# Router on turned tiles of the residual between the output product's last steps, ranks in five wide matmuls, shorter slot sums, and attention evictions between weight splits

## The reference

```python
def first_block(x, ...):
    h = rmsnorm(x, norm1_g)
    u, v_a, q, k, v_b = jnp.split(h @ w_in, splits, axis=-1)
    y_a = chunked_spatial_gating(u, v_a, v_norm_g, w_s, b_s)
    q, k = rmsnorm(q per 64 columns), rmsnorm(k per 64 columns)
    o = rmsnorm(diff_attention(q, k, v_b, lam, slopes), sub_norm_g) * (1.0 - lam_init)
    g_a, g_b = jnp.split(jax.nn.sigmoid(h @ w_gate + b_gate), 2, axis=-1)
    merged = g_a * (y_a @ w_up_a) + g_b * (o @ w_up_b)
    x = x + merged @ w_out
    h2 = rmsnorm(x, norm2_g)
    return x + hierarchical_moe(h2, ...)

def hierarchical_moe(t, w_rg, b_rg, w_re, b_re, w1, w3, w2):   # 4 groups of 8 experts
    g_gate, g_idx = lax.top_k(softmax(t @ w_rg + b_rg), 1)
    e_logits = (t @ w_re + b_re)[the 8 of group g_idx]
    e_w, e_idx = lax.top_k(softmax(e_logits), 2)
    weight = g_gate * e_w / sum(e_w)
    y = sum over the 2 chosen experts of weight * (silu(t @ w1) * (t @ w3)) @ w2
```

## Time and profile before

| what | us |
|---|---|
| median of 3 runs | 1691.47 |
| lowest and highest | 1690.91, 1695.44 |
| the profiled execution | 1695.65 |
| its span, first to last instruction | 1693.9 |
| TensorE busy | 1515.3 (89%) |
| VectorE busy | 935.4 (55%) |
| ScalarE busy | 717.2 (42%) |
| GpSimd busy | 143.3 (8%) |

### The profile page before, as it was taken

The page is one execution under the profiler, slowest core; times in us unless marked ns, Lnnn a source line. Parts: engine busy times, 40 slices in busy tenths (PEclk is TensorE's granted clock), DMA queues, the critical chain, the costliest instruction groups (busy, mean ns, idle before and its releaser), DMA issues.

```text
span 1693.9 us, 17655 instructions
## 1 busy us (share of the span) xinstructions
PE 1515.3 (89%) x7159; PEld 1138.8 (67%) x7159; DVE 935.4 (55%) x1292; ACT 717.2 (42%) x1046; POOL 143.3 (8%) x87
## 2 busy tenths in 40 slices
PE   7999999899899647999999959896978999999999
PEld 5888776677678534555555538675867876678887
DVE  3544237754756356888888846656554453222344
ACT  4333334553452205666677653443221126643221
POOL 0000000000000001444333320000000000000000
PEclk9999989999999867999999989997978977999999
DMA  6222221131232607999999961201010012002231
GB/s 213 75 100 88 87 74 51 50 100 50 75 117 105 220 34 246 312 308 311 310 313 311 308 213 51 75 25 50 1 50 1 1 50 99 1 1 96 89 139 50
DMA packets 76955, 205.40 MB, mean 121 GB/s; under 512 B 10707, under 2 KB 11845, under 8 KB 72774
## 3 DMA queue, kind: packets, MB, share of 16 engines
q1 hardware_dynamic: 70978, 193.70, 33.6%
q0 software_dynamic: 5760, 10.50, 2.4%
q10 hardware_dynamic: 132, 0.03, 0.0%
HBM read 195.81 MB, written 16.78 MB: 125 GB/s over the span
## 4 chain that ended last, share of the span: by engine, by line
PE 63%; DVE 25%; ACT 9%; issue 1%; DMA 1%; SPq 0%; DVEq 0%; POOLq 0%; ACTq 0%
PE PS L501 15%; PE PS L503 15%; PE PS L502 14%; DVE wlo L1158 6%; DVE htlo L1158 5%; PE PS L934 4%; ACT whi L1957 3%; DVE ylo L1158 3%; PE PS L498 2%; PE PS L1083 2%; ACT yhi L1957 2%; ACT hthi L1957 2%; PE PS L1074 2%; ACT work L1957 1%; DVE work L1575 1%
## 5 line engine op out<-in xcount | busy, mean ns | idle before, releaser
L1158 DVE TENSOR_TENSOR wlo<-raw,whi 128x2048 fp32r<-128x2048 f32 x74 | 169.5, 2291 | 333.8 <-ACT whi L1957 333.8
L1957 ACT ACTIVATE whi<-raw 128x2048 fp32r<-128x2048 f32 x74 | 141.5, 1912 | 307.9 <-PE PS L503 296.6
L501 PE MATMUL PS<-hthi,whi 128*128 128x512 f32 x480 | 198.2, 413 | 10.0 <-DVE work L1283 6.4
L501 PE MATMUL PS<-whi,hthi 128*128 128x512 f32 x480 | 199.5, 416 | 8.2 <-ACT work L1957 6.4
L503 PE MATMUL PS<-whi,htlo 128*128 128x512 f32 x480 | 190.2, 396 | 0.0
L502 PE MATMUL PS<-wlo,hthi 128*128 128x512 f32 x480 | 189.9, 396 | 0.0
L503 PE MATMUL PS<-hthi,wlo 128*128 128x512 f32 x480 | 189.2, 394 | 0.0
L502 PE MATMUL PS<-htlo,whi 128*128 128x512 f32 x480 | 189.1, 394 | 0.0
L498 PE MATMUL PS<-consts,work 128*128 128x128 f32 (+1 forms) x652 | 99.1, 295 | 86.0 <-DVE work L1185 31.0
L498 PEld LDWEIGHTS PS<-consts,work 128*128 128x128 f32 (+1 forms) x652 | 83.5, 180 | 116.0 <-DVE work L1185 32.1
L1957 ACT ACTIVATE work<-PS 128x512 f32<-128x512 f32 (+3 forms) x204 | 102.9, 529 | 95.9 <-PE PS L998 53.1
(11 more groups left out here) (318 smaller groups left out, 2704.1 us busy)
## 6 DMA issues: line engine op xcount, KB each, us to landing
raw<-in_w_in SPq DMA_DIRECT2D x44, 1024.0 KB, 5.0
raw<-in_w SPq DMA_DIRECT2D x80, 512.0 KB, 5.7
scratch<-in_w SPq DMA_DIRECT2D x48, 512.0 KB, 6.0
raw<-in_w SPq DMA_DIRECT2D x19, 1024.0 KB, 8.0
scratch<-in_w SPq DMA_DIRECT2D x13, 1024.0 KB, 8.2
raw<-in_w_gate SPq DMA_DIRECT2D x8, 1024.0 KB, 5.1
raw<-in_w_out SPq DMA_DIRECT2D x8, 1024.0 KB, 5.1
raw<-in_w_up_a SPq DMA_DIRECT2D x6, 1024.0 KB, 5.0
```

Of the source, the lines that this page charges most:

```text
L501: e.matmul(o, lh, rh, start=start, stop=False)
L1158: tt(lo, raw_place(j), as_f32(hi), SUB).then_inc(*ve.mark("lo", j))
L1957: return e.activation(o, i, f, bias=bias, scale=scale)
```

## The change

**Attention.** In each half one `split()` (high part on ScalarE, low part on VectorE) now stands ahead of the eviction and norm of `q` and one behind it; the same for `k`. `natural_block("k")` stands ahead of `turn_block("q")` on ScalarE, `natural_block("v")` ahead of `turn_block("k")`, and the last split of the half behind that. The number of splits in a half is the same.

**Router.** `normalise` has no case for the second norm any more. `xs` is written by ScalarE. TensorE turns the residual `x1` itself, tile by tile (`turn_tile`, two banks a tile), from the second column block of the last `wo` unit on, and multiplies each turned tile (as the stationary operand) with `wr` (`router`), which VectorE has multiplied by the gains. The 128 x 144 result is scaled by 1/rms on VectorE and gets the bias there. ScalarE and VectorE evict half a turned tile each.

**Ranks, slots, info.** Ranks come from one matmul with the triangle over 160 columns and four with ones over 128, 96, 64 and 32. Slots come from one table rank + base for all experts, masked once for both picks. The count of extra tiles is a shift. `info` is split in two groups of 8 matmuls, tokens and weights.

**Splits and waits.** Of the four splits beside the output product VectorE makes the one of unit 38 ahead of the residual of its first half, 39 and 40 behind that, and that of unit 41 behind `idx`; ScalarE copies 38, 39 and 40 in a row and 41 behind the second exponential. Load 45 waits for `pe["info weights"]`. `sync` is otherwise as it was.

```diff
@@ tensor
+        def turn_tile(i):
+            on.wait_ge(*ve["out", "wo", 1, i])
+            for a in range(2):
+                ps = fresh("x1t", i, a)
+                for k in range(HB):
+                    m = turn(ps[:, k * P:k * P + P], x1[:, i, (a * HB + k) * P:(a * HB + k + 1) * P])
...
+            for k in range(KD):
+                m = e.matmul(PS[:, bank.of["logits",], of], x1t[i][:, k, :], wr[:, k, :], start=k == 0, stop=k == KD - 1)
...
-        for b in range(2):
-            product("wo", b, False, hthi, htlo, by_k=lambda k: ve["merged", k])
...
+        product("wo", 0, False, hthi, htlo, by_k=merged)
+        for _ in part("wo", 1, 0, False, hthi, htlo, by_k=merged):
+            pass
         fresh("logits")
...
+        second = part("wo", 1, 1, False, hthi, htlo, by_k=merged)
         for i in range(NT):
...
+            for _ in range(HB):
+                next(second)
+            if i:
+                turn_tile(i - 1)
+            if i > 1:
+                router(i - 2)
+        next(second, None)
+        turn_tile(NT - 1)
+        router(NT - 2)
+        router(NT - 1)
...
-        for i in range(NT + 1):
-            for j in range(min(i + 1, NT)):
-                m = e.matmul(rp[:, i, :], upper if j == i else ones, both[:, j, :], start=j == 0,
-                             stop=j == min(i, NT - 1))
+        e.matmul(rp, upper, both5, start=True, stop=False, skip_group_check=True)
+        for j in range(NT):
+            m = e.matmul(rp[:, j + 1:, :], ones, both[:, j, :].unsqueeze(1).broadcast_to([P, NT - j, NE]), start=False,
+                         stop=j == NT - 1, skip_group_check=True)
@@ vector
-        normalise("n2", g2)
-        on.wait_ge(*pe["logits"])
...
+        inverse = inverse_rms("n2", NT, D)
...
+        tt(lg, inside("logits")[:, 0:NT * (NG + NE)].rearrange("p (i n) -> p i n", i=NT),
+           bc(inverse, [P, NT, NG + NE]), MUL).then_inc(*ve.mark("out", "logits"))
...
+        stt(idx[:, :], inside("info")[0:CAP, 0:NTILE], -1.0, beyond, ADD, ADD).then_inc(*ve.mark("out", "info"))
+        ve.also("idx")
+        split()
+        on.wait_ge(*pe["info weights"])
@@ scalar
+            natural_block("k", half, W[:, 3, :], SQ, [ve["q", half, "normed"], ve["dist"], po["dist"]])
             turn_block("q", half, W[:, 1, :], gq8["q1"], [ve["gains"], ve["gated", G_A - 1]])
-            natural_block("k", half, W[:, 3, :], SQ, [ve["q", half, "normed"], ve["dist"], po["dist"]])
             root(f"k{half}", 32)
             split()
             split()
+            natural_block("v", half, W[:, 0, :], None, [pe["turned", "q", half, HB - 1]])
             turn_block("k", half, W[:, 2, :], columns["k1"], [])
-            natural_block("v", half, W[:, 0, :], None, [pe["turned", "q", half, HB - 1]])
+            split()
@@ sync
-        on.wait_ge(*ve["n2", "xs"])
+        on.wait_ge(*ac["n2", "xs"])
```

More of the change, by code:

```diff
@@ L256, in build @@
     ring3 = small(3, 16)
-    info = small(2, NTILE)[0:CAP]
+    info = small(NTILE)[0:CAP]
     ba, dta = small(NT, NB), small(2 * DH)
@@ L773, in tensor @@
         for n in range(2 * NT):
-            m = e.matmul(ps[0:CAP, 0:2 * NTILE], is_place[:, n, :], val[:, n, :], start=n == 0, stop=n == 2 * NT - 1)
+            m = e.matmul(ps[0:CAP, 0:NTILE], is_place[:, n, :], val[:, 0, n, :], start=n == 0, stop=n == 2 * NT - 1)
         m.then_inc(*pe.mark("info"))
         bank.filled(("info",))
+        ps = fresh("info weights")
+        on.wait_ge(*ve["val weights"])
+        for n in range(2 * NT):
+            m = e.matmul(ps[0:CAP, 0:NTILE], is_place[:, n, :], val[:, 1, n, :], start=n == 0, stop=n == 2 * NT - 1)
+        m.then_inc(*pe.mark("info weights"))
+        bank.filled(("info weights",))
         def bring(n):
@@ L2124, in scalar @@
             split()
-            split()
             if half:
@@ L2189, in scalar, with square, turned_tile @@
         merge_second(2, "merged", pe["gb", 1, HB - 1])
-        for b in range(2):
-            split()
-            split()
-        normalise("n2", g2, lambda i: ve["out", "wo", 1, i])
+        split()
+        split()
+        split()
+        use(LOGS)
+        def square(i):
+            on.wait_ge(*ve["out", "wo", 1, i])
+            act(xs[:, i, :], x1[:, i, :], ACT.Square, accum_out=stat["n2"][0][:, i:i + 1]).then_inc(*ac.mark())
+        def turned_tile(i):
+            on.wait_ge(*pe["x1t", i, 0])
+            act(x1t[i][:, 0:HB, :], inside("x1t", i, 0).rearrange("p (k n) -> p k n", k=HB), ACT.Copy).then_inc(
+                *ac.mark("out", "x1t", i, 0))
+        for i in range(NT):
+            square(i)
+            if i == NT - 1:
+                ac.also("squares", "n2")
+            if i:
+                turned_tile(i - 1)
+        turned_tile(NT - 1)
+        root("n2", NT)
+        on.wait_ge(*ve["inverse", "n2"])
+        for i in range(NT):
+            act(xs[:, i, :], x1[:, i, :], ACT.Copy, scale=stat["n2"][1][:, i:i + 1]).then_inc(*ac.mark())
+        ac.also("n2", "xs")
         on.wait_ge(*ve["ex"])
@@ L2573, in load @@
                 on.wait_ge(*ve["overflow"])
-                on.wait_ge(*pe["info"])
+                on.wait_ge(*pe["info weights"])
             for place, src in units[j]:
```

202 lines of the change are left out of this document (98 added, 104 removed).

## The result

The changed kernel takes 1668.63 us (median of 4 runs, 1664.12 to 1669.93) against 1691.19 (4 runs, 1690.16 to 1695.44) for the kernel before on the same chip: ratio 0.9854, 95% interval 0.9826 to 0.9882. The forecast was 1664.1, faster, with a range of 1653 to 1679. The profiled execution took 1669.93 us, its span is 1668.2: 25.7 less than before's 1693.9. (In a row of windows: the stretch, its length, then busy time with instructions of PE, PEld, DVE, ACT and POOL, the granted clock, the DMA share, GB/s.)

The account below looks back on a forecast made before the run. TensorE held 63% of the chain, with four 3.20 us pauses and a serial stretch before the first expert. Attention -18.4 and that stage -9 gave -27.4 us, from 1691.47 to 1664.1 us, range 1653 to 1679.

Parts of the forecast that it names:

- clock given back: Attention: TensorE time lost to a lowered clock behind the pauses, 6.3 us by the rows, taken as 5.9 us.
- low part's end to the norm's write landed: Before the first gather: from unit 41's low part (610.7) to the write landed (625.3), 12.6 us traffic plus 2 ramp.
- from there to the first tokens: First gather: starts 0.6 us after the norm's write lands and takes 6 us, first tokens at 632.
- stage, sum: Output product to first expert: first tokens at 632 instead of 641.0, -9 us, bounds -16 and -3.
- the forecast's second figure: Router matmuls: 107 ns per stationary load by the Trainium skill, 6.8 us for 64; the sum is 0.6 us lower.
- What is late next: Before the first gather: the norm's write, behind load 44 and unit 41's low part, keeps the slot tokens' gain from the gather.
- the 22 of the sum: Whole kernel: -22 us if the gather shares with loads 45 and 46, which adds 5 us.
- (a): Norm's write not held: gather starts at 609, stage gives about 27, in all -46, 1645.5 us; chance 0.07.
- (b): Attention: reordered splits become new waits and lose clock; with half the gain lost -18, 1673 us; chance 0.21.
- (c): Both late ends, attention -11.8 and the gather at 638: -15, 1677 us; chance 0.07.
- (d): Experts' rhythm entered in another phase leaves DMA engines idle every round; at 1.1 us an expert, +8, 1699 us; chance 0.03.
- (e): Experts' rhythm: smaller loss, 0.7 us an expert, cancels most of the gain, within 0.3%; chance 0.03.

Follow-up runs that it names:

- router_only: The changed kernel with the attention part undone (old order of splits and evictions there): 1685.76 us, ratio 0.9951.
- xn_first: The changed kernel with load 44 issued behind the writes of the residual and the norm's result in SyncE's queue: 1647.44 us, ratio 0.9744.
- late_split: The changed kernel with k's second split of half 1 put behind the gate sigmoids (on VectorE, behind gate a's merges): 1675.7 us, ratio 0.9905.
- splits_only: The changed kernel with the old order of evictions in attention, the splits kept in their new places: 1682.18 us, ratio 0.993.
- rank_wait_split: The changed kernel with unit 41's low part made on VectorE in the wait for the ranks, SyncE's queue unchanged: 1657.2 us, ratio 0.9762.
- both_moved: The changed kernel with load 44 behind the writes and unit 41's low part in the wait for the ranks: 1643.78 us, ratio 0.9698.
- ranks_old: The changed kernel with the 14 rank matmuls of the kernel before in place of the five wide ones: 1672.25 us, ratio 0.9896.
- xn_before_x1: The changed kernel with the norm's write ahead of the residual's four, both still behind load 44: 1661.74 us, ratio 0.9824.

## Why the prediction was right, and where it missed

| step | forecast | measured |
|---|---|---|
| four pauses gone | 12.8 | 12.8 |
| clock given back | 5.9 | 6.4 |
| new waits in attention | 0.3 | 0 |
| output product's end later by turns and router | 3.7 | 3.7 |
| turns and router behind it | 7.4 | 7.3 |
| ranks | 2.4 | 2.5 |
| ranks' end to tile numbers | 5.4 | 5.2 |
| slot tokens, beside attention | -27.9 | -28.3 |
| low part's end to the norm's write landed | 14.6 | 16.6 |
| from there to the first tokens | 6.6 | 8.1 |
| stage, sum | -9 | -6.2 |
| whole, in the traces | -27.4 | -25.7 |

**Attention: right.** All four pauses went, and all of their clock: 19.2 for 18.4. What the forecast didn't see is that the clock of before is a matter of chance. In before and `router_only` together five of eight pauses of 3.2 us were followed by half clock, for 1.5 to 2.9 us each. The trace that the forecast read had lost three times out of four, so 5.9 us is on the high side of an average; that this is why it stood 4.2 us above its median is likely, not shown. The changed kernel's trace stands 1.3 above its own, hence 25.7 us between the traces and 22.6 between the medians; the interval of the ratio is 20.0 to 29.4 us. Of the 4.5 us between the forecast of 1664.1 and the measured 1668.6, 1.7 are in the sum and some 2.9 are this difference. The range's bound of -18.9 should have been -19.1 by the forecast's own terms, which moves it by 0.2 us.

**Router, ranks, slots: right in each step** to 0.4 us. The router matmuls, for which no row stood, took 1.71 us for 16 (0.107 each) at full clock, at the lower edge of the 0.11 to 0.12 taken, at the 107 ns of the forecast's second figure, and not near the 0.22 of the nearest row, which ran at half clock.

**What is late next: right in kind, low by 2.8 us in price.** The terms that were too small are the two transfers. The write: 12.6 us of traffic and 2 of ramp. By the GB/s row the ramp lasts 5.6 us, at 129 to 380 before the plateau of 415 to 427, and costs 2.5. At nothing stood the 0.5 us from the low part's end to the first traffic, and about 1 us for traffic of loads 45 and 46, an estimate from the row: it adds up to 5.7 MB by the landing, where load 44 and the writes are 5.2. ("Six issues of 0.4 us" is in no sum. The residual's four took 2.73, not 1.6; whether they held the ramp back is open.) The gather: "the first took 3.8 us with queues empty, ... so I take 6": 7.1 us and 0.9 to its start. Each lies inside its bounds, which is why the range held. The Trainium skill (DMA: Bandwidth & Descriptors, Queues, rings and completion order) says that an engine takes turns between queues. The gather of the changed kernel took 3.4 us more than with empty queues (3.7), not the 5 that all of loads 45 and 46 would need. By the row some 0.7 of their 2.1 MB had moved at its start, and the other 1.4 are 3.4 us at 415 GB/s, an estimate that fits. It fits taking turns as well as standing behind, and no run here tells the two apart. That the median gain of 22.6 is close to the 22 of the sum that has those 5 us in it is chance: in the traces it is 25.7.

**The rivals.** (a) is refuted in the changed kernel by the order in SyncE's queue, and measured as a version: with the write not held it is 1647.4 (`xn_first`; the forecast for that case was 1645.5). (b) has its price, 7 us for the one miss tried (`late_split`), where the forecast gave 9 for half of the gain; it did not happen, and `splits_only` shows such misses (1.11 and 2.41 us) with the old eviction order. (c) did not happen. (d) and (e), the experts' rhythm: the window of 339 us has the same work at 0.90 for 0.92 of the DMA engines, and starts 20 to 50 us earlier in other versions passed to the end without a fixed loss. Between versions the time from first tokens to the end varies from 1047 to 1059 us (the longest in `rank_wait_split`); what sets that spread was not tried.

## What to carry to other kernels

When a stage on the path gets shorter, look for every event that used to be hidden under it, and in each queue for what stands *ahead* of it and what that waits for: here a load that nobody needed yet held a finished write for 23 us (ScalarE's scaled tiles are done at 570.5, the write is issued at 594.1), and moving it gave 18 us, where the whole change had given 23. A pause of TensorE that comes from a bank may take two edits at once, since either alone only shortens it. And a wide VectorE step can be free in a wait: the low part in the wait for the ranks ended at 575.89 and cost the slot tokens nothing. No run shows one that is too long.

## What the runs showed of the hardware

- Half clock after a pause is not certain: 5 of 8 pauses of 3.20 or 3.21 us were followed by it, the one of 3.99, and 2 of 12 between 0.89 and 2.41 (one of 2.15 and the one of 2.41; the other of 2.15 and the shorter ones were not). It cost 1.5 to 3.0 us each time. In three of the eight it fell 0.7 to 1.7 us after TensorE was back, so the first matmul does not tell.
- The first gather's instruction on GpSimd takes 1.01 us, and took 2.91 the one time that VectorE ran a 128 x 2048 subtraction over it (`xn_first`; the 32 gathers of the changed kernel take 0.93 to 1.41). The Trainium skill (GPSIMD Engine Reference, Specifications) says that the two engines share their way into SBUF, and that a VectorE step with two inputs in SBUF, as this one, contends for it. The run agrees with the rule; that the shared way is the reason was not tried apart.
- Executions differ in their first 100 us: with the granted clock at 1.00 there (`both_moved`, `ranks_old`) the first pause on the scores' result stands at 252.6 and 253.2; with 0.98 (the changed kernel, `late_split`) it stands 2 to 3 us later, at 255.4. Single traces must be compared from a common place on, not by their ends.
- The same 2 MB write landed 6.6 us after its issue with nothing around it (`xn_first`), 7.7 in the kernel before, behind the residual's 2 MB issued 6 us ahead, 10.9 behind 1 MB and ahead of 2 MB (`xn_before_x1`), and 13.3 to 14.6 behind 3 MB (the changed kernel, `rank_wait_split` and the others with that order).
